# Splitting keys and queries into rounded parts and rests for the scores of six of eight samples, in a two-layer encoder step

## The reference

```python
q_lat = einsum('bqhn,lhn->bqhl', q_nope, w_uk)
s_past = einsum('bqhl,bkl->bhqk', q_lat, c_ckv) + einsum('bqhr,bkr->bhqk', q_pe, c_kpe)
s_new  = einsum('bqhl,bkl->bhqk', q_lat, ckv)   + einsum('bqhr,bkr->bhqk', q_pe, kpe)
p = softmax(concatenate([s_past, s_new]) * MLA_SCALE)
o_lat = einsum('bhqk,bkl->bqhl', p[past], c_ckv) + einsum('bhqk,bkl->bqhl', p[new], ckv)
```

## Time and profile before

| | |
|---|---|
| median of 3 runs | 1610.16 us (1609.55 to 1610.38) |
| profiled execution, first to last instruction (span) | 1608.3 us |
| PE busy | 1600.9 us (100%) |
| chain that ended last: PE | 98% |
| DVE, ACT, POOL busy | 820.0, 597.6, 268.1 us |
| granted clock of the core | 1.000 |
| sample stage | 361.9 to 410.3 us, 3% of the span |

### The profile page before, as it was taken

One profiled execution on the slowest core, in us unless ns is written; L12 is line 12 of the kernel. 1 busy time (PEld: TensorE's weight loads), 2 busy tenths in 40 slices (PEclk: granted clock), 3 DMA queues, 4 the chain that ended last, 5 costly groups with the idle time before them and its releaser, 6 DMA issues.

```text
span 1608.3 us, 24111 instructions
## 1 busy us (share of the span) xinstructions
PE 1600.9 (100%) x9172; PEld 1532.5 (95%) x9172; DVE 820.0 (51%) x968; ACT 597.6 (37%) x770; POOL 268.1 (17%) x267
## 2 busy tenths in 40 slices
PE   9999999999999999999999999999999999999998
PEld 9999999988999999999999999898989899999987
DVE  6544344864454444445444344674747576444422
ACT  6333222574343333234333223424343354333322
POOL 0111122530121110221111032303030312111000
PEclk9999999999999999999999999999999999999999
DMA  7444344564244443454444345566575755444332
GB/s 218 121 121 130 105 126 135 173 206 148 58 126 130 130 127 94 126 150 131 130 123 120 104 125 186 204 219 228 198 245 172 254 179 147 130 130 130 113 125 103
DMA packets 322273, 238.03 MB, mean 148 GB/s; under 512 B 8560, under 2 KB 287280, under 8 KB 322096
## 3 DMA queue, kind: packets, MB, share of 16 engines
q1 hardware_dynamic: 321936, 236.86, 48.3%
q10 hardware_dynamic: 288, 0.50, 0.1%
HBM read 215.34 MB, written 20.94 MB: 147 GB/s over the span
## 4 chain that ended last, share of the span: by engine, by line
PE 98%; DVE 1%; ACT 1%; issue 0%; DMA 0%; ACTq 0%; DVEq 0%
PE bank L168 26%; PE bank L170 26%; PE bank L169 26%; PE bank L489 2%; PE bank L488 2%; PE bank L487 2%; PE bank L1666 1%; PE bank L1665 1%; PE bank L1664 1%; PE bank L1073 1%; PE bank L396 1%; PE bank L1702 1%; PE bank L1777 1%; PE bank L1733 1%; PE bank L1692 0%; PE bank L917 0%
## 5 line engine op out<-in xcount | busy, mean ns | idle before, releaser
L145 DVE TENSOR_TENSOR WL<-RAW,WH 128x2048 fp32r<-128x2048 f32 (+3 forms) x191 | 401.8, 2105 | 296.3 <-ACT WH L138 295.6
L138 ACT ACTIVATE WH<-RAW 128x2048 fp32r<-128x2048 f32 (+3 forms) x191 | 330.0, 1730 | 561.9 <-PE bank L170 479.5
L168 PE MATMUL bank<-XH,WH 128*128 128x384 f32 x1368 | 458.4, 335 | 0.0
L170 PE MATMUL bank<-XH,WL 128*128 128x384 f32 x1368 | 457.1, 334 | 0.0
L169 PE MATMUL bank<-XL,WH 128*128 128x384 f32 x1368 | 457.0, 334 | 0.0
L168 PEld LDWEIGHTS bank<-XH,WH 128*128 128x128 f32 x1368 | 256.8, 188 | 3.4 <-issue 3.1
L169 PEld LDWEIGHTS bank<-XL,WH 128*128 128x128 f32 x1368 | 256.8, 188 | 0.2
L170 PEld LDWEIGHTS bank<-XH,WL 128*128 128x128 f32 x1368 | 256.8, 188 | 0.0
L653 POOL TENSOR_TENSOR si<-si,rsb 128x384 f32<-128x384 f32 x88 | 94.3, 1072 | 626.4 <-ACT si L524 591.8
L168 PE MATMUL bank<-AH,WH 128*128 128x384 f32 x528 | 176.4, 334 | 0.0
L169 PE MATMUL bank<-AL,WH 128*128 128x384 f32 x528 | 176.4, 334 | 0.0
(11 more groups left out here) (307 smaller groups left out, 1960.3 us busy)
## 6 DMA issues: line engine op xcount, KB each, us to landing
RAW<-w_ffn_gate_dram SPq DMA_DIRECT2D x86, 512.0 KB, 4.0
RAW<-w_ffn_up_dram SPq DMA_DIRECT2D x86, 512.0 KB, 5.2
RAW<-w_ret_in_dram SPq DMA_DIRECT2D x48, 512.0 KB, 4.8
RAW<-w_ffn_down_dram SPq DMA_DIRECT2D x48, 384.0 KB, 4.0
st<-state_ret_dram SPq DMA_DIRECT2D x32, 512.0 KB, 6.9
new_state_sample_dram<-st SPq DMA_DIRECT2D x32, 512.0 KB, 6.6
RAW<-w_ffn_down_dram SPq DMA_DIRECT2D x48, 320.0 KB, 3.3
RAW<-w_ffn_down_dram SPq DMA_DIRECT2D x22, 512.0 KB, 4.3
```

Of the source, the lines that this page charges most:

```text
L138: ins = act.activation(dst(WH), src, ACT.Copy)
L145: ins = dve.tensor_tensor(dst(WL), src, dst(WH).bitcast(F32), ALU.subtract)
L168: pe.matmul(ps, wh, xh, start=first, stop=False)
L170: return pe.matmul(ps, wl, xh, start=False, stop=last)
```

## The change

Samples 0 and 1 keep their f32 scores. For samples 2 to 7 (`SPLIT = 2`):

- ACT copies the whole key tile (two latent tiles and the rotated one, 3 x 528 = 1584 columns, loaded and new) to fp32r (`keys_hi`), into one of two tiles `key_hi`. It waits for the load, for POOL's new keys, and from sample 4 on for the scores of b - 2, which read the same tile. `keys_hi(2)` and the rounded queries (`queries_hi`, `rot_q`, 768 columns each) stand ahead of `mixed(7)`; `keys_hi(b + 3)` stands behind the exponentials of b, for b = 0 to 4; a second `queries_hi` (768 columns) follows `keys_hi(4)`.
- DVE subtracts (`key_lo`, 1584 columns, in the place of the key tile), for sample b + 2 between the negative maximum of b and the sum of b.
- POOL subtracts the queries' rests (`queries_lo`: 256 columns for each sample, and once 768 columns on 64 partitions), and its new keys come one sample earlier.
- PE does, for each of the two banks, per latent tile high x high, high x low and low x high, and for the rotated part two products: 8 products a bank, 16 a sample. The rotated keys are stacked twice on 128 rows; the queries have their rounded part on rows 0 to 63 and their rest on 64 to 127.
- The keys of a sample come in one transfer of 768 KB in place of one of 512 KB and one of 128 KB. The order and the waits of `sp_attention` stay.
- The buffers are placed anew (`key_hi` and `rot_q` over `qp` and `wukT`), and pairs of semaphores become one with higher counts (`m_max`, `m_smax`, `m_sinv`, `ones_set`, `eps_set`); what each wait waits for stays the same.

```diff
             def load_keys(self, sp, b):
-                sp.dma_start(ktc[b % N_KT][:, :, 0:PAST_LEN], a["ckvT"][b]).then_inc(sem(f"kt_in{b % N_KT}"), 16)
-                sp.dma_start(ktp[b % N_KT][:, 0:HP], a["kpeT"][b]).then_inc(sem(f"kt_in{b % N_KT}"), 16)
+                sp.dma_start(keys_in[b % N_KT][:, :, 0:PAST_LEN], a["keysT"][b]).then_inc(sem(f"kt_in{b % N_KT}"), 16)
...
             def sample_scores(self, pe, b):
+                if b < SPLIT:
+                    pe.wait_ge(sem(f"kt_in{b}"), 16)
+                    pe.wait_ge(sem("m_kt_new"), 2 * (b + 1))
+                else:
+                    pe.wait_ge(sem("m_key_lo"), b - SPLIT + 1)
+                    pe.wait_ge(sem("m_query_lo"), b - SPLIT + 2)
...
+                if b >= SPLIT:
+                    n, hi, lo = b - SPLIT, key_hi[b % 2], key_lo[b % N_KT]
+                    for ps, cols in ((sa, slice(HP, KEYS)), (sb_, slice(0, HP))):
+                        for t in range(KV):
+                            pe.matmul(ps, lat_hi[:, t, n, :], hi[:, t, cols], start=(t == 0), stop=False)
+                            pe.matmul(ps, lat_hi[:, t, n, :], lo[:, t, cols], start=False, stop=False)
+                            pe.matmul(ps, lat_lo[:, t, b, :], hi[:, t, cols], start=False, stop=False)
+                        pe.matmul(ps, rot_q[:, n, :], hi[:, KV, cols], start=False, stop=False)
+                        pe.matmul(ps, rot_q[:, n, :], lo[:, KV, cols], start=False, stop=True).then_inc(sem("m_sscores"), 1)
+                    return
...
+                def keys_hi(b):
+                    act.wait_ge(sem(f"kt_in{b % N_KT}"), 16 * (b // N_KT + 1))
+                    act.wait_ge(sem("m_kt_new"), 2 * (b + 1))
+                    if b == SPLIT:
+                        act.wait_ge(sem("m_scores"), MLA_HEADS)
+                        act.wait_ge(sem("m_qps"), DEC_BATCH)
+                    elif b >= SPLIT + 2:
+                        act.wait_ge(sem("m_sscores"), 2 * (b - 1))
+                    act.activation(key_hi[b % 2][:, :, :], keys_in[b % N_KT][:, :, :], ACT.Copy).then_inc(sem("m_split"), 1)
...
                 turned(MLA_HEADS - 1)
+                keys_hi(SPLIT)
+                act.wait_ge(sem("m_lat"), 4 * KV)
+                queries_hi(SPLIT, SPLIT + 3)
+                act.activation(rot_q[:, :, :], ...).then_inc(sem("m_split"), 1)
                 mixed(MLA_HEADS - 1)
...
                         act.activation(ps_[:, b % 2, dst], src, ACT.Exp, ...).then_inc(sem("m_sexp"), 1)
+                    if SPLIT + b + 1 < DEC_BATCH:
+                        keys_hi(SPLIT + b + 1)
+                    if b == 1:
+                        queries_hi(SPLIT + 3, DEC_BATCH)
...
+                    if b < N_SPLIT:
+                        n = b + SPLIT
+                        dve.wait_ge(sem("m_split"), (1, 4, 5, 7, 8, 9)[b])
+                        dve.tensor_tensor(key_lo[n % N_KT][:, :, :], keys_in[n % N_KT][:, :, :], key_hi[n % 2][:, :, :].bitcast(F32),
+                                          ALU.subtract).then_inc(sem("m_key_lo"), 1)
                     dve.wait_ge(sem("m_sexp"), 3 * (b + 1))
...
+                def queries_lo(b):
+                    n = b - SPLIT
+                    if n == 0:
+                        pool.wait_ge(sem("m_split"), 3)
+                        pool.wait_ge(sem("m_kt_new"), 2 * (SPLIT + 2))
+                        pool.tensor_tensor(rot_q[ROPE:P, :, :], qps[ROPE:P, SPLIT:, :, :]..., ALU.subtract).then_inc(sem("m_query_lo"), 1)
...
+                    pool.tensor_tensor(lat_lo[:, :, b, :], lat[:, :, b, :, :]...,
+                                       lat_hi[:, :, n, :].bitcast(F32), ALU.subtract).then_inc(sem("m_query_lo"), 1)
```

More of the change, by code:

```diff
@@ L302, in start_pool @@
         def start_pool(pool):
-            pool.memset(ones, 1.0).then_inc(sem("ones_set"), 1)
-            pool.memset(root_y[:, 3:4], EPS).then_inc(sem("eps_set"), 1)
+            pool.memset(ones, 1.0).then_inc(sem("consts_set"), 1)
+            pool.memset(root_y[:, 3:4], EPS).then_inc(sem("consts_set"), 1)
         def start_dve(dve):
@@ L706, in stream_kernel @@
         KW = HP + DEC_SEQ
-        KT = KV * (PAST_LEN + DEC_SEQ)
+        KEYS = PAST_LEN + DEC_SEQ
+        KT = (KV + 1) * KEYS
+        SPLIT = 2
+        N_SPLIT = DEC_BATCH - SPLIT
         MASK_ROW = (ROPE, ROPE + 32)
@@ L711, in stream_kernel @@
             mcos, msin = mtab[:, 0:T], mtab[:, T:2 * T]
-            shared = sb("shared", [P, MLA_HEADS * T + KV * D_MODEL], F32, r)
+            widths = (MLA_HEADS * T + KV * D_MODEL, MLA_HEADS * T + MLA_HEADS * KV_LORA, 2 * KT, KV * DEC_BATCH * MLA_HEADS * DEC_SEQ)
+            with ExitStack() as r0:
+                whole = sb("whole", [P, sum(widths)], F32, r0)
+            with ExitStack() as r0:
+                split = sb("split", [P, sum(widths)], F32R, r0)
+            (shared, late, kt, lat), (shared_r, late_r, kt_r, lat_r) = (
+                [x[:, sum(widths[:i]):sum(widths[:i + 1])] for i in range(4)] for x in (whole, split))
+            r.enter_context(nc.sbuf_tensor("whole_held", [P, sum(widths)], F32))
             qn = shared[:, 0:MLA_HEADS * T].rearrange("p (h n) -> p h n", h=MLA_HEADS)
@@ L715, in stream_kernel @@
             ps_ = shared[:, 0:2 * (PAST_LEN + P)].rearrange("p (s n) -> p s n", s=2)
-            qp = sb("qp", [P, MLA_HEADS, T], F32, r)
+            qp = late[:, 0:MLA_HEADS * T].rearrange("p (h n) -> p h n", h=MLA_HEADS)
+            wukT = late[:, MLA_HEADS * T:].rearrange("p (h n) -> p h n", h=MLA_HEADS)
             kall = sb("kall", [P, KV + 1, T], F32, r)
@@ L719, in stream_kernel, with key_tiles @@
             tok = sb("tok", [P, KV_LORA], F32, r)
[L720 to L724, removed]
+            def key_tiles(kt, shared):
+                places = (kt[:, 0:KT], kt[:, KT:], shared[:, MLA_HEADS * T:MLA_HEADS * T + KT])
+                return [x.rearrange("p (t n) -> p t n", t=KV + 1) for x in places]
+            keys_in, key_lo = key_tiles(kt, shared), key_tiles(kt_r, shared_r)
+            N_KT = len(keys_in)
+            key_hi = [late_r[:, i * KT:(i + 1) * KT].rearrange("p (t n) -> p t n", t=KV + 1) for i in range(2)]
+            rot_q = late_r[:, 2 * KT:2 * KT + N_SPLIT * P].rearrange("p (b n) -> p b n", b=N_SPLIT)
+            lat_hi = shared_r[:, 2 * (PAST_LEN + P):2 * (PAST_LEN + P) + KV * N_SPLIT * P].rearrange("p (t b n) -> p t b n", t=KV, b=N_SPLIT)
+            lat_lo = lat_r.rearrange("p (t b n) -> p t b n", t=KV, b=DEC_BATCH)
+            lat = lat.rearrange("p (t b h q) -> p t b h q", t=KV, b=DEC_BATCH, h=MLA_HEADS)
             wuv = sb("wuv", [P, KV, D_MODEL], F32, r)
-            wukT = sb("wukT", [P, MLA_HEADS, KV_LORA], F32, r)
             qps = sb("qps", [P, DEC_BATCH, MLA_HEADS, DEC_SEQ], F32, r)
-            lat = sb("lat", [P, KV, DEC_BATCH, MLA_HEADS, DEC_SEQ], F32, r)
             with ExitStack() as r1:
@@ L1044, in sample_scores @@
                 pe.matmul(sb_, q1, latent[:, 1, 0:HP], start=False, stop=False)
-                pe.matmul(sa, qr[0:ROPE, :], rotated[0:ROPE, :], start=False, stop=True).then_inc(sem("m_sscores"), 1)
+                pe.matmul(sa, qr[0:ROPE, :], rotated[0:ROPE, HP:], start=False, stop=True).then_inc(sem("m_sscores"), 1)
                 pe.matmul(sb_, qr[ROPE:P, :], rotated[ROPE:P, 0:HP], start=False, stop=True).then_inc(sem("m_sscores"), 1)
@@ L1205, in act, with queries_hi @@
                         part_hi(act, c, c % 2, c // 2, i % 2)
+                def keys_hi(b):
[7 more added lines that the diff above has]
+                    act.activation(key_hi[b % 2][:, :, :], keys_in[b % N_KT][:, :, :], ACT.Copy).then_inc(sem("m_split"), 1)
+                def queries_hi(lo, hi):
+                    act.activation(lat_hi[:, :, lo - SPLIT:hi - SPLIT, :],
+                                   lat[:, :, lo:hi, :, :].rearrange("p t b h q -> p t b (h q)"), ACT.Copy).then_inc(sem("m_split"), 1)
                 sample_queries(2)
@@ L1209, in act @@
                 turned(MLA_HEADS - 1)
+                keys_hi(SPLIT)
+                act.wait_ge(sem("m_lat"), 4 * KV)
+                queries_hi(SPLIT, SPLIT + 3)
+                act.activation(rot_q[:, :, :], qps[:, SPLIT:, :, :].rearrange("p b h q -> p b (h q)"), ACT.Copy).then_inc(sem("m_split"), 1)
                 mixed(MLA_HEADS - 1)
@@ L1444, in pool, with new_keys @@
                         pool.tensor_copy(qps[row:row + ROPE, b:b + 2, :, :], sample[0:ROPE, b:b + 2]).then_inc(sem("m_qps"), 1)
-                for b in range(DEC_BATCH):
-                    pool.wait_ge(*((sem("m_zero"), b) if b else (sem("m_qps"), DEC_BATCH)))
+                def new_keys(b):
                     if b >= N_KT:
@@ L1451, in pool, with zeros @@
                     new = slice(SEQ + b * DEC_SEQ, SEQ + (b + 1) * DEC_SEQ)
-                    pool.tensor_copy(ktc[b % N_KT][:, :, PAST_LEN:], ckvT[:, :, new]).then_inc(sem("m_kt_new"), 1)
```

(29 more changed lines are left out.)

36 lines of the change are left out of this document (17 added, 19 removed).

## The result

The changed kernel takes 1630.26 us (median of 4 runs, 1628.41 to 1631.53), the kernel before beside it 1610.15 (1609.55 to 1610.38): 20.1 us more, a ratio of 1.0126 with a 95% interval of 1.0114 to 1.0138. It is slower. The forecast was 1626 with a range of 1612 to 1632; the size came out 4 us above the forecast. Times are medians of fast executions; one of nine in a single run, that on the start, took 1975.30 us at a granted clock of 0.752 and is left out.

The account below looks back on a forecast made before the run. PE was taken as the bound, busy 1600.9 of 1608.3 us. Late key loads in ACT's queue cost 17.2, shorter periods return 1.3: span 1608.3 + 15.9 = 1624.2, plus 1.9 to the median, 1626 us; range 1612 to 1632.

Parts of the forecast that it names:

- The products: PE's scores: 16 products a sample take 1.97 us, period 4.74 in place of 5.41, 4.0 us less over six samples.
- The new work of ACT: ACT's copies: keys_hi with 1584 columns takes 1.5 us, a queries_hi or rot_q 0.85.
- The walk along ACT's queue: ACT's list: late key loads behind keys_hi hold the work after it; turn(4) starts at 405.2, 17.2 us late.
- 15.9: Net delay of the sample stage: turn(4) 17.2 us late, less 1.3 given back by two shorter periods.
- the two long landings: Keys of 6 and 7: from SP's issue to the landing 6.1 us each, bounds 4.87 and 6.9.
- clock rival: PE at half clock after 6.2 us gaps: 2.4 us more behind turn(4), none behind the first; 1628.5 us, chance 0.22.
- DVE and POOL at 0: Subtractions: DVE's key_lo 1.9 us, POOL's 0.7 and 2.1, counted as 0 on the path.
- The loads are in time: Key loads land before ACT asks; only waits for the scores of b - 2 and at turn(1) remain: 1613, chance 0.12.
- PE's saving counts: ACT's copies hide wholly behind mix(b - 2) and 4.0 us come off PE: 1606, chance 0.07.

Follow-up runs that it names:

- the wait put into the kernel before: Kernel before, with ACT waiting behind the exponentials of b (0 to 4) until the keys of b + 3 have landed: 1621.66 us.
- the loads in time: Changed kernel, SP issuing the keys of 6 and 7 ahead of its waits for m_olat 1 and 2: 1616.64 us.
- the later place of the copies: Changed kernel, keys_hi(b + 2) on ACT behind turned_probs(b - 2) and ahead of the exponentials of b: 1622.93 us.
- the last load moved too: Changed kernel, SP issuing the keys of 5, 6 and 7 ahead of the cached latents of 4, key copies one place later on ACT: 1608.33 us.
- the run with PE kept busy: Changed kernel, with 24 extra f32 products of 128 columns behind mix(1) and 28 behind mix(2): 1628.01 us.
- both orders: Changed kernel, with SP's earlier issue of the keys of 6 and 7 and keys_hi one place later on ACT: 1611.19 us.
- the last version: Changed kernel, keys of 5 to 7 loaded ahead of the latents of 4, samples 3 to 7 split, keys of 3 copied behind turned_probs(0): 1607.70 us.
- the start reordered: As both orders, with DVE's subtractions for 2 and 3 moved behind sample 1's negative maximum and scaling, keys_hi(3) behind its exponentials: 1613.09 us.

## Why the prediction was right, and where it was short

**The products.** Forecast 1.97 us for the 16 products. Six of them at full clock, in the timeline of the changed kernel:

```profile
386.07 0.28 PE L1064 MATMUL bank<-split 128*128 128x272 f32 x1
386.19 0.29 PE L1065 MATMUL bank<-split 128*128 128x272 f32 x1
386.32 0.29 PE L1063 MATMUL bank<-split 128*128 128x272 f32 x1
...
387.07 0.28 PE L1064 MATMUL bank<-split 128*128 128x256 f32 x1
387.19 0.28 PE L1065 MATMUL bank<-split 128*128 128x256 f32 x1
387.30 0.28 PE L1063 MATMUL bank<-split 128*128 128x256 f32 x1
```

They start every 0.125 us at 272 columns and every 0.118 at 256 (forecast 0.126 and 0.120), and a period without a wait is 4.75 (forecast 4.74). Right. (The upper bound of the 16 products, at 0.173 each, is 2.77 us and not 2.78.)

**The new work of ACT.** `keys_hi` takes 1.52 us (1.5), 768 columns 0.83 (0.85). Right.

**The walk along ACT's queue.** Its places beside the forecast:

| | forecast | measured |
|---|---|---|
| `keys_hi(3)` starts | 369.5 | 368.77 |
| turn(1) | 376.0 | 375.23 |
| exponentials of 3 | 383.2 | 385.11 |
| start of the exponentials of 3 to SP's issue | 2.61 | 2.95 (388.06) |
| from that issue to `keys_hi(6)` | 6.1 | 5.62 (393.68) |
| exponentials of 4 to SP's issue | 2.61 | 2.61 (395.75 to 398.36) |
| from that issue to `keys_hi(7)` | 6.1 | 7.27 (405.63) |
| turn(4) | 405.2 | 407.95 |

The exponentials of 3 to SP's issue took 0.34 us more than forecast because the scaling between them took 0.89 us (0.55 for the next sample), while POOL subtracted.

The mechanism is shown from three sides: the wait put into the kernel before costs 11.6 us, the loads in time take 13.6 off the changed kernel, and the later place of the copies takes 7.3. The last two overlap, since both together bring 19.1 (1630.26 - 1611.19) and not 20.9; with the last load moved too it is 21.9 (1630.26 - 1608.33).

**The clock** is the term that was sized wrongly. The forecast left it out, and the rival had it at one place, behind turn(4), for 2.4 us. There it cost 1.6: 6.30 us between turns 4 and 5 in place of 4.74. Behind turn(3) it cost nothing, as the rival said: PE was done near 403.4 and waited for ACT until 407.95. But it also fell behind the first wait, of 3.17 us at turn(1), which the walk had (a turn 4.2 us late) without asking what PE's clock would do: from 375.23 to the end of the scores of 3 near 382.8, 7.5 us, in place of 4.74. There `keys_hi(5)` waited for these scores, so the 2.8 us were on the path. No edit tested this place by itself, but the profiled execution of the run with PE kept busy is the same up to it, had the same wait, and kept its clock:

```profile
375.02 0.30 PE L1082 MATMUL bank<-ident,whole 128*128 128x128 f32 x1 [3.17 <-ACT psT L1268]
...
382.39 0.30 PE L1082 MATMUL bank<-ident,whole 128*128 128x128 f32 x1 [2.44 <-ACT psT L1268]
```

From turn(1) to turn(2) it took 7.37 us, the changed kernel 10.14 (375.23 to 385.37): 2.8 us for the clock at this place.

The two places make 2.8 + 1.6 = 4.4 us, and 15.9 + 4.4 = 20.3, where 20.1 was measured. That this fits so closely is partly luck, as the table shows: turn(1) came 0.8 us early, the first of the two long landings was 0.5 short and the steps from `keys_hi(6)` to the exponentials of 4 0.2, while SP's first issue was 0.3 late and the second landing 1.2 long. These misses cancel. So forecast and clock rival were both partly right: one mechanism, with the other on top.

**DVE and POOL at 0.** Here the price was wrong and the cover held. The first subtraction of the keys took 3.25 us on DVE, beside POOL's two, of which the second took 2.17 for 256 columns; alone they take 1.80 and 0.73. The second took 2.37 us beside one of POOL. The timelines of DVE and POOL:

```profile
365.12 3.25 DVE L1417 TENSOR_TENSOR split<-whole,split 128x1584 fp32r<-128x1584 f32 x1
...
370.66 2.37 DVE L1417 TENSOR_TENSOR split<-whole,split 128x1584 fp32r<-128x1584 f32 x1
```

```profile
364.88 1.82 POOL L1524 TENSOR_TENSOR split<-qps,split 64x768 fp32r<-64x768 f32 x1 [0.42 <-ACT split L1256]
366.78 2.17 POOL L1529 TENSOR_TENSOR split<-whole,split 128x256 fp32r<-128x256 f32 x1
...
370.63 0.74 POOL L1529 TENSOR_TENSOR split<-whole,split 128x256 fp32r<-128x256 f32 x1
```

The first one held the scaling of 0 and made PE wait 1.7 us at turn(0), in the shadow of the longer wait at turn(1). With the later place of the copies PE waits for DVE's scaling at turn(1) instead, 1.88 us with both orders. The version with five samples split has no key work ahead of turn(1) on DVE and waits 1.01 there; how much of its gain comes from this is not shown.

**The rivals of the forecast.** "The loads are in time" had 1613; with SP's order changed the kernel takes 1616.64, at the lower clock between 376 and 381 us (0.51); less the 2.8 us of that place it is 1613.8, an estimate. So its walk was sound, and its condition did not hold in the change as made. "PE's saving counts" (1606) named its condition, copies that never hold a turn; the last version comes near it, 1607.7 with five samples.

What stays open: why the transfer of the keys of 7 took 6.87 us from its issue and that of 6 only 5.22, with the same neighbour in the queue. It is not the sample: in the run with the later place on ACT the copy of the keys of 6 started 6.68 us after their issue (383.82 to 390.50) and that of 7 only 5.41 (395.46 to 400.87). Open is also 0.6 us by which the span grew less than the stage came late (the output products start at 430.49 in place of 410.27, 20.2 us, the span grew by 19.6), though the stage also started 0.5 us earlier.

## What to carry to other kernels

A new consumer on an in-order engine moves the moment at which its data is needed: before a copy or a wait is put into such a list, look up where its load is issued, what that issue waits for, and what stands behind the copy. If the load hangs on work that follows the same place in the list, the engine pays the way to the issue and the transfer in full in each such turn. And where the walk gives PE a gap, give the work behind the gap a price at both levels of the clock.

## What the runs showed of the hardware

- PE came back at the lower clock level from waits of 2.96 us (0.50, the start reordered) to 6.60 us (0.50 from 394.7 to 399 us, the later place on ACT), but not always. Behind the 3.17 us at turn(1) the stretch from 376 to 381 us had a clock of 0.50 in the changed kernel and 0.51 with SP's order changed; in the run with PE kept busy later, behind the same wait of the same length, it was 1.00:

```profile
376.00:381.00 5.00, 3.95 (x34) 3.75 (x33) 2.81 (x8) 1.00 (x2) 1.35 (x4) 1.00 0.00 1
```

  This is also a likely source of the spread of the changed kernel's runs, 3.1 us, against 0.8 of the kernel before; that was not tested by itself. Shorter waits are no safe ground either: with the keys first, PE ran at 0.56 from 369 to 371 us behind a wait of 1.66 us, and at 1.00 behind 1.67 us with both orders.
- Where a subtraction on DVE and one on POOL overlap, the one that starts later pays. POOL's first took 1.82 us, as it does with DVE idle (1.81 with the start reordered); DVE's behind it 3.25 in place of 1.80, POOL's next 2.17 in place of 0.73. Each later one ends about its usual time after the earlier one's end: 366.70 + 1.80 = 368.50 (368.37 measured), 368.37 + 0.73 = 369.10 (368.95), and for the next pair 371.37 + 1.80 = 373.17 (373.03).
- The clock column shows the fall here (0.50), while it stood at 1.00 over the slow records at the program's start, 0.234 us each in place of 0.112.
